# Seven block products in place of eight for twelve pairs of weight units in the third and fourth up stages

## What is computed

```python
def conv_ffn(h, w_up, conv_w, conv_b, w_down):
    u = h @ w_up                      # 1024 -> 2 * 2816
    up = jnp.pad(u, ((0, 0), (CONV_WIDTH - 1, 0), (0, 0)))
    conv = conv_b
    for j in range(CONV_WIDTH):       # three taps along the tokens
        conv = conv + conv_w[j] * up[:, j:j + s]
    a, g = jnp.split(conv, 2, axis=-1)
    return (jax.nn.silu(a) * g) @ w_down
```

## Time and profile before

| What | Value |
|---|---|
| time, median of 3 runs | 2323.34 us (2322.82 to 2324.22) |
| span of the profiled execution | 2320.9 us |
| TensorE busy | 2309.1 us, 99% |
| TensorE weight loads | 1950.9 us, 84% |
| VectorE busy | 1498.3 us, 65% |
| ScalarE busy | 1119.0 us, 48% |
| GpSimd busy | 223.6 us, 10% |
| granted TensorE clock | 1.000 (2.4 GHz) |

### The profile page before, as it was taken

The page is one execution under the profiler, slowest core; times in us unless marked ns, Lnnn a source line. Parts: engine busy times, 40 slices in busy tenths (PEclk is TensorE's granted clock), DMA queues, the critical chain, the costliest instruction groups (busy, mean ns, idle before and its releaser), DMA issues.

```text
span 2320.9 us, 32131 instructions
## 1 busy us (share of the span) xinstructions
PE 2309.1 (99%) x12088; PEld 1950.9 (84%) x12088; DVE 1498.3 (65%) x2173; ACT 1119.0 (48%) x1829; POOL 223.6 (10%) x313
## 2 busy tenths in 40 slices
PE   9999999999999999999999999999999999999999
PEld 8777889988888888999888778888888878888887
DVE  6665789952738968899428876777434456777731
ACT  6655544452539965445326854444323444544420
POOL 1221013200125410232000000000001000000000
PEclk9999999999999999999999999999999999999999
DMA  5433223332242222333322223323322323233232
GB/s 167 152 132 102 85 92 109 104 112 93 87 118 64 64 84 82 99 110 111 113 89 77 64 82 91 100 90 106 100 93 91 100 69 95 91 100 100 95 107 79
DMA packets 72541, 226.30 MB, mean 98 GB/s; under 512 B 7921, under 2 KB 19489, under 8 KB 72417
## 3 DMA queue, kind: packets, MB, share of 16 engines
q1 hardware_dynamic: 67840, 210.72, 28.5%
q0 software_dynamic: 4576, 13.89, 1.9%
HBM read 221.28 MB, written 2.18 MB: 96 GB/s over the span
## 4 chain that ended last, share of the span: by engine, by line
PE 92%; DVE 3%; ACT 3%; POOL 1%; issue 1%; DMA 0%; DVEq 0%; ACTq 0%; SPq 0%
PE bank L338 26%; PE bank L340 25%; PE bank L339 25%; PE bank L478 5%; PE bank L470 4%; PE bank L1605 1%; PE bank L1596 1%; PE bank L1639 1%; DVE w_lo L312 0%; DVE h L756 0%; POOL hgrn_lv L2560 0%; PE bank L2651 0%; PE bank L2015 0%; POOL hgrn_lv L2547 0%; PE bank L3103 0%
## 5 line engine op out<-in xcount | busy, mean ns | idle before, releaser
L312 DVE TENSOR_TENSOR w_lo<-raw,w_hi 128x1024 fp32r<-128x1024 f32 (+1 forms) x310 | 402.3, 1308 | 218.4 <-ACT w_hi L307 218.1
L338 PE MATMUL bank<-x_hi,w_hi 128*128 128x512 f32 x1344 | 529.2, 394 | 1.2 <-ACT sb_q L2761 1.0
L340 PE MATMUL bank<-x_hi,w_lo 128*128 128x512 f32 x1344 | 523.4, 389 | 0.0
L339 PE MATMUL bank<-x_lo,w_hi 128*128 128x512 f32 x1344 | 523.1, 389 | 0.0
L307 ACT ACTIVATE w_hi<-raw 128x1024 fp32r<-128x1024 f32 (+1 forms) x310 | 344.6, 1121 | 179.9 <-PE bank L340 93.5
L338 PEld LDWEIGHTS bank<-x_hi,w_hi 128*128 128x128 f32 x1344 | 252.3, 188 | 57.4 <-issue 3.1
L340 PEld LDWEIGHTS bank<-x_hi,w_lo 128*128 128x128 f32 x1344 | 252.2, 188 | 53.0
L339 PEld LDWEIGHTS bank<-x_lo,w_hi 128*128 128x128 f32 x1344 | 252.5, 188 | 51.2 <-issue 0.5
L338 PE MATMUL bank<-st_a_hi,w_hi 128*128 128x512 f32 (+1 forms) x396 | 145.1, 366 | 0.0
L340 PE MATMUL bank<-st_a_hi,w_lo 128*128 128x512 f32 (+1 forms) x396 | 144.7, 365 | 0.0
L1374 DVE TENSOR_TENSOR bank<-bank,rstd 128x512 f32<-128x512 f32 x120 | 83.2, 696 | 92.2 <-PE bank L340 92.2
(11 more groups left out here) (444 smaller groups left out, 4673.2 us busy)
## 6 DMA issues: line engine op xcount, KB each, us to landing
raw<-in_w_up SPq DMA_DIRECT2D x120, 512.0 KB, 3.5
raw<-in_w_down SPq DMA_DIRECT2D x64, 704.0 KB, 4.2
st_raw_even<-in_w_up SPq DMA_DIRECT2D x28, 512.0 KB, 4.2
st_raw_odd<-in_w_up SPq DMA_DIRECT2D x24, 512.0 KB, 4.0
raw<-in_w_fox_qk SPq DMA_DIRECT2D x16, 512.0 KB, 3.7
raw<-in_w_hgrn_qf SPq DMA_DIRECT2D x16, 512.0 KB, 3.5
fox_c_keys_a<-fox_c_rows POOLq DMA_DIRECT2D x8, 640.0 KB, 4.1
fox_c_keys_b<-fox_c_rows POOLq DMA_DIRECT2D x8, 640.0 KB, 4.5
```

The source lines that it names most:

```text
L312: nc.vector.tensor_tensor(w_lo[:, slot, 0:size], raw[:, slot % 2, 0:size], w_hi[:, slot, 0:size].bitcast(F32), ALU.subtract).then_inc(sem( ...
L338: nc.tensor.matmul(out, w[0], x[0], start=first, stop=False)
L339: nc.tensor.matmul(out, w[0], x[1], start=False, stop=False)
L340: return nc.tensor.matmul(out, w[1], x[0], start=False, stop=last)
```

## The change

In the third and fourth up stages, tiles 0 to 9 (20 units) stay in the old form, written out without the hardware loop. Tiles 10 to 21 (12 pairs) take seven block products. The differences from the form of the first two stages:

- Sums of products are made by TensorE in PSUM. Product 0 of a pair goes to a half bank; ScalarE copies it out (`cv_act_copy`, "first"); product 2 is added on top, copied again ("second"); product 4 on top, then product 6 on top. Products 1 and 3 go to the halves of another bank, and 5 is added on 3 after ScalarE has copied 3 out negated (`cv_act_m5`). VectorE makes the first row of results with one addition of 512 columns (`cv_dve_c1`) and one quarter with a subtraction of 256 (`cv_dve_c22`); ScalarE copies the last quarter out negated (`cv_act_c21`).
- The results lie in SBUF (`st_out`), so the taps read SBUF instead of PSUM.
- TensorE's order interleaves three pairs (`cv_order`).
- There is no rstd scaling for these pairs, since the forms are made from the normalised input. The forms are made by VectorE and ScalarE during tiles 2 to 7.
- The splits into `a_hi` and `a_lo` for all 22 tiles move behind the last pair. The down stage takes its first two units piecewise.
- SyncE fetches the first two down units by waits on `cv_lo_g` and `cv_c22`.

```diff
-        def mm3(out, w, x, first, last):
-
-            nc.tensor.matmul(out, w[0], x[0], start=first, stop=False)
-            nc.tensor.matmul(out, w[0], x[1], start=False, stop=False)
-            return nc.tensor.matmul(out, w[1], x[0], start=False, stop=last)
+        def mm3(out, w, x, first, last, onto=False):
+            nc.tensor.matmul(out, w[0], x[0], start=first, stop=False, skip_group_check=onto)
+            nc.tensor.matmul(out, w[0], x[1], start=False, stop=False, skip_group_check=onto)
...
+        def cv_sum_bank(n):
+            return ps[(6, 7, 3)[n % 3]][:, HALVES[0]]
+        def cv_row_bank(n):
+            return ps[4 + n % 2]
+        def cv_order():
+            order = [(0, 0)]
+            for k in range(CV_PAIRS):
+                order += [(k, 2), (k, 1)]
+                if k:
+                    order.append((k - 1, 6))
+                order.append((k, 3))
+                if k < CV_PAIRS - 1:
+                    order.append((k + 1, 0))
+                order += [(k, 4), (k, 5)]
+            return order + [(CV_PAIRS - 1, 6)]
+        CV_ORDER = cv_order()
+        CV_AT = {at: i + 1 for i, at in enumerate(at for at in CV_ORDER if at[1] != 6)}
+        def cv_done(eng, f, n, i):
+            if i == 6:
+                used(eng, u_of(f"up{f}") + 2 * (CV_FIRST + n) + 1)
+            else:
+                wait(eng, "cv_part", 6 * CV_PAIRS * (f - 2) + CV_AT[n, i])
+        def cv_pe(pe, f, n, i):
+            g = CV_PAIRS * (f - 2) + n
+            a, first = cv_sum_bank(n), i in (0, 1, 3)
+            if i == 0:
+                if n == 0:
+                    wait(pe, "cv_xlo", 7 * (f - 2) + 7)
+                if n == 2:
+                    pe.wait_ge(sem("gated_ready"), FT * f + CV_FIRST + 2)
+                if n >= 3:
+                    wait(pe, "cv_c21", g - 2)
+                wait(pe, "cv_lo_a", g + 1)
+            elif i == 2:
+                wait(pe, "cv_first", g + 1)
+                wait(pe, "cv_lo_s12", g + 1)
+            elif i == 6:
+                wait(pe, "cv_c22", g + 1)
+                wait(pe, "cv_lo_g", g + 1)
+            elif i == 1:
+                if n >= 2:
+                    wait(pe, "cv_c1", g - 1)
+            elif i == 4:
+                wait(pe, "cv_second", g + 1)
+                wait(pe, "cv_lo_s3", g + 1)
+            elif i == 5:
+                wait(pe, "cv_m5", g + 1)
+                wait(pe, "cv_lo_s4", g + 1)
+            out = {1: cv_row_bank(n)[:, HALVES[0]], 3: cv_row_bank(n)[:, HALVES[1]], 5: cv_row_bank(n)[:, HALVES[1]]}.get(i, a)
+            for k in range(QUAD):
+                w = [st_w(n, h, slice(i, i + 1))[:, 0, k * P:(k + 1) * P] for h in range(2)]
+                ins = mm3(out, w, [cv_form_hi[i][:, k, :], cv_form_lo[i][:, k, :]], first and not k, k == QUAD - 1, True)
+            if i == 6:
+                ins.then_inc(sem("unit_used"), 2)
+            else:
+                ins.then_inc(sem("cv_part"), 1)
...
-                bodies(pe, f"up{f}", up_body, first=4)
-                pe.wait_ge(sem("gated_ready"), FT * f + FT - 1 + 2)
+                for n, i in CV_ORDER:
+                    cv_pe(pe, f, n, i)
...
+        def cv_act_hi(act, f, n, blocks):
+            g = CV_PAIRS * (f - 2) + n
+            if blocks == "a":
+                st_raw_wait(act, f, n, 0)
+                if n > 1:
+                    cv_done(act, f, n - 2, 1)
+            elif blocks == "s12":
+                wait(act, "cv_sum1", g + 1)
+            elif blocks == "s3":
+                wait(act, "cv_pool3", g + 1)
+            elif blocks == "g":
+                st_raw_wait(act, f, n, 1)
+            else:
+                wait(act, "cv_sum2", g + 1)
+            src, at = cv_block(n, blocks)
+            nc.scalar.activation(st_w(n, 0, at), src, ACT.Copy).then_inc(sem("cv_hi_" + blocks), 1)
+        def cv_act_copy(act, f, n, step):
+            cv_done(act, f, n, 2 * step)
+            nc.scalar.activation(cv_pu[n % 2][:, step, :], cv_sum_bank(n), ACT.Copy).then_inc(
+                sem("cv_second" if step else "cv_first"), 1)
+        def cv_act_c21(act, f, n):
+            cv_done(act, f, n, 6)
+            nc.scalar.activation(st_out[:, 2, :], cv_sum_bank(n), ACT.Copy, scale=-1.0).then_inc(sem("cv_c21"), 1)
+        def cv_act_m5(act, f, n):
+            cv_done(act, f, n, 3)
+            if n:
+                wait(act, "cv_c22", CV_PAIRS * (f - 2) + n)
+            nc.scalar.activation(cv_minus5[:], cv_row_bank(n)[:, HALVES[1]], ACT.Copy, scale=-1.0).then_inc(sem("cv_m5"), 1)
...
+        def cv_act_a_hi(act, f, ks):
+            for k in ks:
+                if k < 20 and k % 4 == 0:
+                    cv_done(act, f, CV_PAIRS - 1, (0, 2, 1, 3, 4)[k // 4])
+                elif k == 20:
+                    cv_done(act, f, CV_PAIRS - 1, 5)
+                act.wait_ge(sem("gated_ready"), FT * f + k + 1 + 2)
+                nc.scalar.activation(a_early[:, k, :], a_plain(k), ACT.Copy).then_inc(sem("ahi_ready"), 1)
+        def act_conv(act, f):
+            last = CV_PAIRS - 1
+            down = following[f"up{f}"]
+            cv_act_copy(act, f, 0, 0)
+            cv_act_hi(act, f, 1, "a")
+            for k in range(CV_PAIRS):
+                if k:
+                    cv_act_tap(act, f, k - 1, 0)
+                cv_act_copy(act, f, k, 1)
+                if k < last:
+                    cv_act_hi(act, f, k + 1, "s12")
+                if k:
+                    cv_act_c21(act, f, k - 1)
+                    cv_act_tap(act, f, k - 1, 1)
+                cv_act_m5(act, f, k)
+                if k:
+                    cv_act_silu(act, f, k - 1)
+                if k < last:
+                    cv_act_hi(act, f, k + 1, "s3")
+                if k < last:
+                    cv_act_copy(act, f, k + 1, 0)
+                    cv_act_hi(act, f, k + 1, "g")
+                    cv_act_hi(act, f, k + 1, "s4")
+                if k < last - 1:
+                    cv_act_hi(act, f, k + 2, "a")
+            act.sem_inc(sem("hi_ready"), 2 * CV_PAIRS)
+            convert_act(act, 0, down.first, down.size)
+            cv_act_a_hi(act, f, range(0, 10))
+            convert_act(act, 1, down.first + 1, down.size)
+            cv_act_a_hi(act, f, range(10, 16))
+            cv_act_tap(act, f, last, 0)
+            cv_act_c21(act, f, last)
+            cv_act_tap(act, f, last, 1)
+            cv_act_a_hi(act, f, range(16, 18))
+            cv_act_silu(act, f, last)
+            cv_act_a_hi(act, f, range(18, FT))
...
+            for n in range(CV_PAIRS if f >= 2 else 0):
+                g = CV_PAIRS * (f - 2) + n
+                ra, rg = st_raw_pair(n)
+                st_raw_wait(pool, f, n, 1)
+                if n:
+                    wait(pool, "cv_lo_s12", g)
+                else:
+                    wait(pool, "cv_xlo", 7 * (f - 2) + 7)
+                nc.gpsimd.tensor_tensor(st_sum[:, 1, :], rg[:, 0, :], rg[:, 1, :], ALU.add).then_inc(sem("cv_pool1"), 1)
+                st_raw_wait(pool, f, n, 0)
+                if n:
+                    wait(pool, "cv_lo_s3", g)
+                nc.gpsimd.tensor_tensor(st_third[:, 0, :], ra[:, 0, :], rg[:, 0, :], ALU.add).then_inc(sem("cv_pool3"), 1)
...
+        def cv_dve_sum(dve, f, n, second):
+            g = CV_PAIRS * (f - 2) + n
+            ra, rg = st_raw_pair(n)
+            if not second:
+                st_raw_wait(dve, f, n, 0)
+                wait(dve, "cv_pool1", g + 1)
+                if n:
+                    wait(dve, "cv_lo_s4", g)
+                nc.vector.tensor_tensor(st_sum[:, 0, :], st_sum[:, 1, :], ra[:, 0, :], ALU.add).then_inc(sem("cv_sum1"), 1)
+            else:
+                wait(dve, "cv_lo_s12", g + 1)
+                nc.vector.tensor_tensor(st_sum[:, 0, :], st_sum[:, 0, :], ra[:, 1, :], ALU.add).then_inc(sem("cv_sum2"), 1)
+        def cv_dve_c1(dve, f, n):
+            g = CV_PAIRS * (f - 2) + n
+            cv_done(dve, f, n, 5)
+            wait(dve, "cv_first", g + 1)
+            wait(dve, "cv_second", g + 1)
+            nc.vector.tensor_tensor(st_out[:, 0:2, :], cv_pu[n % 2][:], cv_row_bank(n)[:].rearrange("p (b x) -> p b x", b=2),
+                                    ALU.add).then_inc(sem("cv_c1"), 1)
+        def cv_dve_c22(dve, f, n):
+            cv_done(dve, f, n, 4)
+            wait(dve, "cv_m5", CV_PAIRS * (f - 2) + n + 1)
+            if n:
+                dve.wait_ge(sem("conv_ready"), 2 * (FT * (f - 2) + CV_FIRST + n))
+            nc.vector.tensor_tensor(st_out[:, 3, :], cv_minus5[:], cv_sum_bank(n), ALU.subtract).then_inc(sem("cv_c22"), 1)
...
+        def dve_conv(dve, f):
+            last = CV_PAIRS - 1
+            down = following[f"up{f}"]
+            for k in range(CV_PAIRS):
+                if k:
+                    cv_dve_c1(dve, f, k - 1)
+                if k < last:
+                    cv_dve_lo(dve, f, k + 1, "a")
+                    cv_dve_sum(dve, f, k + 1, False)
+                if k:
```

(75 more changed lines are left out.)

208 lines of the change are left out of this document (143 added, 65 removed).

## The result

The changed kernel takes 2391.5 us (median of 4 runs, 2390.4 to 2393.4), the kernel before 2323.7 on the same chip (2322.8 to 2324.2): ratio 1.0295, 95% interval 1.0280 to 1.0309. It is 67.9 us slower. The forecast was 48 us slower, with a range up to 2384, so the direction was right and the time fell above the range, in the 8% of rival E.

The account below looks back on a forecast made before the run. TensorE bounds the kernel before, VectorE's rounds the changed pairs. Per stage -9.5 array, +20.8 entry and rounds, +13.0 end give 24.2 us; twice, 48.4, on 2323.3 makes 2371.7, said as 2371; own range 2360 to 2384.

Parts of the forecast that it names:

- rival E: Time above 2384 us, because TensorE's clock falls in the waits or ScalarE's copies come late for TensorE; chance 8%.
- the array's saving: TensorE's block products in the third and fourth up stages save 0.80 us per pair, 9.6 for 12 pairs, 19.2 in both.
- tiles 0 to 9: VectorE's added 16.4 us before tile 7 in each changed stage costs 0, as VectorE has idle time; bound 3 per stage.
- ninth `a_lo`: Down stage: TensorE idles from 20.5 to 28.2 us after product 5 of pair 10, until VectorE ends this low part.
- end: After product 5 of pair 10, waits for the last subtraction and for the ninth low part lose 13.0 us per stage.
- D: The forecast itself: both GpSimd sums hold VectorE in each round; own range 2360 to 2384 us, chance 55%.
- VectorE's round: VectorE's work for one changed pair: 9.8 us plus 2.2 for GpSimd's sums, 12.05 (bounds 9.8 and 12.4), bounding TensorE.
- the two holds: In each round GpSimd's two sums hold a VectorE tap and gate, which read SBUF, by 1.1 us each.
- B: GpSimd's sums hold up nothing; rounds go by TensorE's 10.08 us, 6.4 more per stage: 2336 us, chance 12%.
- C: One of GpSimd's two sums per round is hidden; round 10.94 us, 12 more per stage: 2347 us, chance 20%.
- The entry: At pair 0 TensorE's second product waits 4.1 us for ScalarE's copy; VectorE's first round ends at 15.5 us.
- The granted clock ... I take 0: Whole kernel: the cost of a clock lowered by the waits is not in the rows and is taken as 0.

Follow-up runs that it names:

- the cheapest run: Changed kernel with GpSimd's sums and VectorE's work on the forms cut to 8 columns, early copy, early subtraction and new end order: 2317.1 us, ratio 0.9978 to the kernel before.

## Where the prediction was right and where it failed

The loss taken apart from the array's timeline, in us per stage. A wait is as its row gives it. "Slow" is the sum of the steps above 0.2267 and 0.12 per matmul, less the waits. The forecast's terms are sums over stretches, so each stretch has its sum.

| term | third | fourth | forecast |
|---|---|---|---|
| the array's saving | -9.6 | -9.6 | -9.6 |
| tiles 0 to 9: waits | 2.8 | 2.8 | |
| tiles 0 to 9: slow | 2.1 | 2.2 | |
| **tiles 0 to 9** | 5.0 | 5.0 | 0 |
| entry: wait for ScalarE's copy | 6.6 | 7.0 | |
| waits in the rounds, eight | 12.8 | 12.7 | |
| entry and rounds: slow | 3.9 | 4.8 | |
| **entry and rounds**, to the end of product 5 of pair 10 | 23.3 | 24.4 | 20.8 |
| product 6 of the last pair | 5.0 | 5.0 | 5.2 |
| ninth `a_lo` | 5.5 | 5.1 | 7.7 |
| last pair and down stage: slow | 3.9 | 4.9 | |
| **end** | 14.4 | 14.9 | 13.0 |
| sum | 33.0 | 34.7 | 24.2 |

33.0 + 34.7 is 67.7, as is the difference of the spans. The 19.3 us that the forecast lacks are, rounded, 10.0 in tiles 0 to 9, 6.1 in entry and rounds, and 3.3 at the ends. The step of the forecast that failed is the first of these: tiles 0 to 9 taken as 0 with a bound of 3 per stage. An estimate from this table: with tiles 0 to 9 at their forecast the time would be 10.0 less, 2381.5, inside the range; the run without VectorE's work on the forms has just these tiles back at their old length and took 2376.1. No rival named this wait: D had up to 3 per stage for these tiles, and E is about the clock and ScalarE's copies.

- **The array's saving, VectorE's round, the two holds: right.** 12.05 forecast, 11.97 found, 10.04 without GpSimd, 11.03 with its sums on VectorE. The rule of the Trainium skill (GPSIMD Engine Reference, Key points) that GpSimd and VectorE contend when VectorE has two SBUF inputs, weighed in the forecast, is borne out by the two runs on GpSimd's sums. Rivals B and C are out.
- **The entry: right in kind, wrong in size.** The forecast let the last scaling of tile 9 start 2.4 us after the first block product, charging 1.1 for GpSimd; it starts 5.1 after (1515.37 against 1510.24). The queue ahead of it, with GpSimd's sum at 1510.59:

```profile
1506.40 1.69 DVE L1593 TENSOR_TENSOR st_sum<-st_sum,st_raw_even 128x512 f32<-128x512 f32 x1 [1.24 <-POOL st_sum L1476]
1509.22 1.23 DVE L1582 TENSOR_TENSOR st_w_even<-st_sum,st_w_even 128x1024 fp32r<-128x1024 f32 x1 [1.13 <-ACT st_w_even L1247]
1510.37 0.69 DVE L1725 TENSOR_TENSOR bank<-bank,rstd 128x512 f32<-128x512 f32 x1
1510.59 1.29 POOL L1476 TENSOR_TENSOR st_sum<-st_raw_first 128x512 f32<-128x512 f32 x1 [3.05 <-DVE st_w_even L1582]
1510.96 1.47 DVE L1596 TENSOR_TENSOR st_sum<-st_sum,st_raw_even 128x512 f32<-128x512 f32 x1
...
1513.69 1.75 DVE L1582 TENSOR_TENSOR st_w_even<-st_sum,st_w_even 128x512 fp32r<-128x512 f32 x1
1515.37 0.69 DVE L1725 TENSOR_TENSOR bank<-bank,rstd 128x512 f32<-128x512 f32 x1
```

  Behind the first block product stand the scaling at 1510.37, a sum at 1510.96 that the forecast left out, and two holds (1.47, 1.75) where it charged one. Ahead of it stand a third hold (1.69) and two idle times (1.24 for GpSimd, 1.13 for ScalarE's high part), so VectorE was late already. The array so idled 6.6 and 7.0, not 4.1. VectorE's first round ended 18.7 us after the first block product (1528.98) instead of 15.5. These 3.2 us, less a little for the shorter rounds, are the miss of the third stage: product 5 of pair 10 ends 134.2 us after the first block product (135.3 in the fourth), not 131.7.
- **The end: right in kind, 1.4 and 1.9 too small.** The wait for the subtraction was 5.0 (forecast 5.2). The ninth `a_lo` was overrated by 2.2 to 2.6: 5.5 and 5.1, not 7.7. The slow matmuls behind the two waits, 3.9 and 4.9, more than fill this up. That ScalarE's tap is late behind its high parts and the second down unit, as the forecast said, stands in the rows.
- **"Tiles 0 to 9 ... I take 0": failed.** They cost 5.0 us per stage, outside even the bound of 3. The reasoning divided VectorE's idle time evenly over ten tiles, while the added work is packed: 9.3 of 10 us in the windows from 1460 and from 1470. And it asked when the array needs a bank, two to four tiles later. The wait isn't for a bank but for the low part of the weights of unit 13. First the kernel before, then the changed one:

```profile
1456.89 1.22 DVE L312 TENSOR_TENSOR w_lo<-raw,w_hi 128x1024 fp32r<-128x1024 f32 x1
...
1468.34 1.21 DVE L326 TENSOR_TENSOR w_lo<-raw,w_hi 128x1024 fp32r<-128x1024 f32 x1
```

  Before, it was done at 1458.11 for a unit that began at 1466.96, 8.9 us ahead. The change brought it 11.4 us later, to 1469.55, and the array stood 2.4 us. The forecast's own "falls behind by some 8 us" set against these 8.9 would have shown how near it was.
- **"The granted clock ... I take 0": failed, but smaller than the slow matmuls look.** The rows "slow" add up to some 9.9 and 11.8 us per stage. Of this 13.1 us, in 99 matmuls, are steps at the lower level of the clock: 2.8 in tiles 0 to 9 (in the 10.0 above), 3.8 at the entries, 6.5 at the ends. The other 8.6 are at full clock and are mostly what each wait costs above its own length: 0.26 us at a wait of 1.6, so 2.1 per stage in the rounds. The entries' part is mostly absorbed by VectorE's pace, and the tiles' part went with their wait in the run without the forms' work; filling the waits gave 5.3 in all.

The chance of 8% for rival E was too low: the forecast had three waits of 4 to 8 us on the array per stage and no row of what the clock does behind such a wait, and treated the absence as zero instead of as an unknown with one sign.

## What to carry to other kernels

When a change trades the array's work for work on VectorE, walk VectorE's queue with the step of each instruction, and add 1.1 us for each GpSimd sum that falls beside two-SBUF-input work; here this gave the round to within 1%. Idle time averaged over a stage doesn't show that added work is covered: lay the work into the tile where it runs, beside what is due there first, here a low part with 8.9 us to spare. A wait of several us on a busy array costs more than itself, as the matmuls behind it are slower; price it, and bound it above when no row shows it. And ask early what the change would bring if every new wait were free: here the array's saving is 19.2 us of 2322, and the cheapest run, with work left out, kept 5 of them.

## What the hardware showed

The granted clock fell behind waits of 5 to 7 us (0.77 in the windows of the entry and of the last pair) and behind one of 2.4 (0.83), while with waits of 1.6 us in each round it stayed at 1.00 (all of 1530 to 1640). Behind the long waits matmuls ran at the lower level, 1.2 GHz. The entry's, and those behind the ninth `a_lo`:

```profile
1518.47 0.58 PE L352 MATMUL bank<-cv_form_hi,st_w_even 128*128 128x256 f32 x1 [6.63 <-ACT cv_pu L1252]
...
1519.07 0.42 PE L354 MATMUL bank<-cv_form_hi,st_w_even 128*128 128x256 f32 x1
1519.28 0.41 PE L352 MATMUL bank<-cv_form_hi,st_w_even 128*128 128x256 f32 x1
...
1672.67 0.80 PE L352 MATMUL bank<-st_a_hi,w_hi 128*128 128x512 f32 x1 [5.50 <-DVE st_a_lo L1642]
1673.27 0.63 PE L353 MATMUL bank<-st_a_lo,w_hi 128*128 128x512 f32 x1
1673.69 0.63 PE L354 MATMUL bank<-st_a_hi,w_lo 128*128 128x512 f32 x1
```

The steps are 0.213 for 256 columns (0.12 at full clock) and 0.427 for 512 (0.2267): not quite double. Behind the wait of 2.36 us in tile 6 the array first goes on at its old pace, and seven steps of 0.427 begin only 1.5 us after the wait has ended (at 1471.20). The Trainium skill (TensorE: Matmul & The Clock Gate, Wait — 56ns, not 53.3ns?) gives 426.7 ns from start to start for 512 columns at the lower clock; the trace agrees. Two rows of the entry's queue show both sides of the hold: the scaling at 1510.37, which reads a bank, keeps its 0.69 beside a GpSimd sum that starts at 1510.59, and the sum at 1510.96, from SBUF alone, takes 1.47. And taps that read SBUF (0.75) were no shorter than those that read a bank.
